# Operands of the token mixer turned by transposing DMA in 16-bit halves instead of by TensorE

## The chip, the cores and the metric

One core of one Trainium2 chip runs the whole program; the metric is device time in microseconds, the median of several runs. Kernel before: 970.59 us, median of 3 runs (971.54, 965.90, 970.59).

## The reference, cut to what matters

Two layers, each `x += 1/2 FFN1; x += mixer; x += 1/2 FFN2`, on x of 256 tokens by 1024 channels, float32; a last RMSNorm follows. The part around the change is the mixer:

```python
h  = rmsnorm(x, norm_mix[l]);  proj = h @ w_in[l]
dq, dk, dv, rq, rk, rv, rg = split(proj)      # dq, dk, dv, (rq|rk), rv, rg: 512 columns each
# group A: 4 heads, two softmax maps each, over q k^T with an ALiBi bias
s = einsum('bhcqd,bhckd->bhcqk', q, k) * scale + bias ; p = softmax(where(causal, s, -inf))
o_diff = head_rms((p[:,0] - lam * p[:,1]) @ v) * g * (1 - lam_init)
# group B: retention, 4 heads, over rq rk^T with a decay per head; gated by silu(rg)
x = x + concat(o_diff, silu(rg) * o_ret) @ w_out[l]
```

q k^T contracts over the 64 channels of a head, so TensorE needs q and k with channels on the partitions, while the projection leaves them with tokens on the partitions. Each of dq, dk and the retention pair (rq|rk) is therefore a [256 tokens x 512] float32 matrix that has to be turned, in two halves of 128 tokens (`tt` = 0, 1), four 128x128 blocks in each.

## The kernel before, in words

The order of the work is written out by hand, one instruction stream for each engine, tied by counting semaphores. SyncE (`sp`) loads weight pieces of 128x2048 float32 (1 MB; some of the last ones are 128x1024) in a ring of three raw buffers: a load waits until VectorE is through with the piece three before it (`lo_done`). ScalarE rounds each piece to its high part (`split_hi`, line 356), VectorE subtracts to get the low part (`split_lo`, line 582), and TensorE makes each product in three matmuls (lines 853 to 855) of 128x512. The mixer's column groups are c = 0 to 5 (dq, dk, dv, rqk, rv, gate); `block_of(c, tt)` is 24 matmuls into the PSUM bank `gu[tt]`, and may only start when ScalarE has read the bank's last use (`read_proj`, line 484, which counts `proj_read`).

In the mixer, ScalarE's stream goes: pieces 2 and 3, `read_proj(0, 0)`, piece 4, `read_proj(0, 1)`, piece 5, `read_proj(1, 0)`, piece 6, `read_proj(1, 1)`, piece 7, `read_proj(2, 0)`, piece 8, `read_proj(2, 1)`, and then the softmax exponentials between further pieces. VectorE makes the low parts of the same pieces. TensorE turns the four halves of dq and dk in the middle of blocks (1,0), (1,1), (2,0) and (2,1): the helper `qk_T` calls `transposes` (line 977), four 128x128 transposes into `tp[tt]`; VectorE copies each to `qT` or `kT` (`read_qkT`, line 709). Then `scores(0)` and `scores(1)` (line 988) come, and blocks (3,0), (3,1). The two halves of rqk are turned in the same way ahead of block (4,1), eight transposes in all, and are used after that block (lines 1046 and 1047).

The FFNs already turn their hidden activations by DMA: GpSimd parts a float32 tile of 128x256 into two planes of 16-bit words (`turn_out`, line 256, a copy of 128x512 uint16), ScalarE's queue issues a transposing DMA (`turn`, line 415), and GpSimd joins the turned planes again (`turn_back`, line 262). In the mixer GpSimd has nothing to do but a few narrow operations.

Of the kernel before, what the change touches and what calls it, by code (L numbers as in the profile page):

```python
# [17 lines left out]
U16 = mybir.dt.uint16  # L18
# [3 lines left out]
P = 128  # L22
D, SEQ, DEPTH = 1024, 256, 2
TT = SEQ // P
# [4 lines left out]
HEADS = 4  # L29
# [10 lines left out]
PROJ = 6  # L40
# [13 lines left out]
def build(nc, x_in, norm_ffn1, w1_gate, w1_up, w1_down, norm_mix, w_in, lam_q1, lam_k1, lam_q2, lam_k2,  # L54
          subln, w_out, norm_ffn2, w2_gate, w2_up, w2_down, norm_final, out):
    ctx = ExitStack()
    with ctx:
# [3 lines left out]
        def sem(name):  # L61
            return ctx.enter_context(nc.semaphore(name))
# [12 lines left out]
        hid = sb("hid", [P, 1024])  # L75
# [12 lines left out]
        halves = kT[:, 0:2, :].rearrange("p a n -> p (a n)").bitcast(U16).rearrange("p (t h n) -> p t h n", t=TT, h=2)  # L88
        halvesT = kT[:, 2:4, :].rearrange("p a n -> p (a n)").bitcast(U16).rearrange("p (t h n) -> p t h n", t=TT, h=2)
        hidT = qT[:, 2:4, :]  # L90
        lams = qT[:, 0:2, :].rearrange("p a (b n) -> p (a b) n", b=2)
        gsub2 = sb("gsub2", [P, DEPTH, V])
        gsub = sb("gsub", [P, V])
# [8 lines left out]
        dq_dk = wide  # L102
# [41 lines left out]
        halves_done, hidT_done, dT_hi_done, dT_lo_done = (sem(n) for n in ("halves_done", "hidT_done", "dT_hi_done", "dT_lo_done"))  # L144

        proj_ready, proj_read = sem("proj_ready"), sem("proj_read")
        qkT_psum, qkT_done = sem("qkT_psum"), sem("qkT_done")
        scores_ready, max_done, negmax_done, exp_done, rec_steps, probs_part, probs_done = (
            sem(n) for n in ("scores_ready", "max_done", "negmax_done", "exp_done", "rec_steps", "probs_part", "probs_done"))
        probsT_psum, probsT_done, pv_ready, o_sq_done, o_rstd_done, o_done = (  # L150
# [85 lines left out]
        def _(pool):  # L236
            def entry(q, tt):

                pool.wait_ge(sq_done, TT * q + tt + 1)
                nc.gpsimd.tensor_scalar(tmp[:, tt:tt + 1], ssq[:, tt:tt + 1], 1.0 / D, EPS, ALU.mult, ALU.add).then_inc(rstd_tmp, 1)  # L240
                pool.wait_ge(rstd_tmp, TT * q + tt + 1)
                nc.gpsimd.tensor_tensor(rstd[:, tt:tt + 1], tmp[:, tt:tt + 1], neg_half[:, 0:1], ALU.pow).then_inc(rstd_done, 1)
# [81 lines left out]
            for l in range(DEPTH):  # L324
                nc.gpsimd.tensor_scalar(gsub2[:, l, :], gsub2[:, l, :], 1.0 - LAM_INIT[l], None, ALU.mult).then_inc(lam_sums, 1)

            def mixer_and_ffn2_entry(layer):
                for tt in range(TT):
                    entry(3 * layer + 1, tt)
                for pair in range(2):  # L330
                    head_factor(layer, pair, o_sq_done, 2 * layer + pair + 1, o_rstd_done)
                for tt in range(TT):
                    head_factor(layer, 2 + tt, ro_sq_done, 2 * layer + tt + 1, ro_rstd_done)
                for tt in range(TT):
                    entry(3 * layer + 2, tt)
# [16 lines left out]
        def _(act):  # L352
# [125 lines left out]
            def mixer(layer):  # L478
                def read_proj(c, tt, dst, func=ACT.Copy):
                    if tt == 0:  # L480
                        act.wait_ge(proj_ready, PROJ * layer + c + 1)
                    else:
                        act.wait_ge(slot_free, SLOTS + LP * layer + MIX0 + (2 * c + 2 if c < PROJ - 1 else W0))
                    nc.scalar.activation(dst, gu[tt][:, :], func, scale=rstd[:, tt:tt + 1]).then_inc(proj_read, 1)

                def exps(h):
                    act.wait_ge(negmax_done, HEADS * layer + h + 1)
                    for t, (a, b) in enumerate(((0, 256), (256, 384))):
                        for c in range(2):
                            i = (h % 2) * 4 + 2 * t + c  # L490
                            ins = nc.scalar.activation(z(h, c, a, b), z(h, c, a, b), ACT.Exp, bias=nmx[:, i:i + 1],  # L491
                                                       accum_out=sums[:, i:i + 1])
                    ins.then_inc(exp_done, 1)

                def read_probsT(h):
                    act.wait_ge(probsT_psum, HEADS * layer + h + 1)
                    nc.scalar.activation(probsT(h, 0, 384), tp[h % 2][:, 0:384], ACT.Copy).then_inc(probsT_done, 1)
# [5 lines left out]
                def prep(pos, n=PIECE):  # L503
                    split_hi(layer, MIX0 + pos, 0, n)

                act.wait_ge(rstd_done, TT * (3 * layer + 1) + TT)
                prep(2)
                for c, dst in enumerate((dq_dk[:, :, 0:512], dq_dk[:, :, 512:1024], dv[:, :, :])):
                    for tt in range(TT):
                        prep(2 * c + 3 + tt)  # L510
                        read_proj(c, tt, dst[:, tt, :])
                act.wait_ge(lam_sums, 7)
                own = bass.ds(2 * layer, 2)
                nc.scalar.activation(lam_exp[:, own], lam_dot[:, own], ACT.Exp).then_inc(lam_exped, 1)
                for tt in range(TT):
                    prep(9 + tt, PIECE if tt == 0 else PIECE // 2)
                    exps(tt)
                    read_proj(3, tt, rqk[:, tt, :])
                read_probsT(0)
                read_probsT(1)  # L520
                for tt in range(TT):
                    prep(11 + tt, PIECE // 2)
# [56 lines left out]
        def _(dve):  # L579
# [123 lines left out]
            def mixer(layer):  # L703
                def prep(pos, n=PIECE):
                    split_lo(layer, MIX0 + pos, 0, n)

                def read_qkT(n, dst):
                    dve.wait_ge(qkT_psum, 6 * layer + n + 1)
                    nc.vector.tensor_copy(dst, tp[n % 2][:, :].rearrange("p (k n) -> p k n", k=4)).then_inc(qkT_done, 1)

                def biased_max(h):

                    dve.wait_ge(scores_ready, HEADS * layer + h + 1)
# [44 lines left out]
                    dve.wait_ge(mT_hi_done, 4 * layer + n + 1)  # L758
                    lo_of(dst, src[:, :].rearrange("p (k n) -> p k n", k=4), hi, mT_lo_done)

                for n in (2, 3, 4):
                    prep(n)
                for n, t in enumerate((qT, qT, kT, kT)):
                    prep(5 + n)
                    read_qkT(n, t[:, :, (n % 2) * P:(n % 2 + 1) * P])
                biased_max(0)
                biased_max(1)
                dve.wait_ge(lam_exped, layer + 1)
# [9 lines left out]
                    dve.wait_ge(probsT_psum, HEADS * layer + h - 1)  # L778
                    biased_max(h)
                prep(11, PIECE // 2)  # L780
                for tt in range(TT):
                    read_qkT(4 + tt, rT[:, :, tt * P:(tt + 1) * P])
                probs(2)
                prep(12, PIECE // 2)
                probs(3)
# [64 lines left out]
        def _(pe):  # L850
# [114 lines left out]
            def mixer(layer):  # L965
# [14 lines left out]
                def four(src):  # L980
                    return [src[:, i * P:(i + 1) * P] for i in range(4)]
# [29 lines left out]
                            todo.append((bank[:, (2 * t + hh) * V:(2 * t + hh + 1) * V], pairs))  # L1011
                    causal(todo, pv_ready)

                def qk_T(c, tt):

                    pe.wait_ge(proj_read, n_read + 2 * c - 1 + tt)
                    if c == 2:
                        pe.wait_ge(qkT_done, 6 * layer + tt + 1)
                    transposes(tp[tt], four(dq_dk[:, tt, (c - 1) * 512:c * 512]), qkT_psum)

                block_of(0, 0, lambda: enter_T(q, 1))
                block_of(0, 1)
                for c in (1, 2):
                    for tt in range(TT):
                        block_of(c, tt, lambda: qk_T(c, tt))
                pe.wait_ge(qkT_done, 6 * layer + 4)
                scores(0)
                scores(1)
# [5 lines left out]
                    pe.wait_ge(negmax_done, HEADS * layer + h - 1)  # L1034
                    scores(h)
                block_of(4, 0)
                for tt in range(TT):
                    pe.wait_ge(proj_read, n_read + 7 + tt)
                    pe.wait_ge(probsT_done, HEADS * layer + tt + 1)
                    transposes(tp[tt], four(rqk[:, tt, :]), qkT_psum)  # L1040
                block_of(4, 1)
                pe.wait_ge(qkT_done, 6 * layer + 6)
                pe.wait_ge(negmax_done, HEADS * layer + 4)
                for h in range(HEADS):
# [2 lines left out]
                    nc.tensor.matmul(acc[h][:, SEQ:384], rT[rows, 2 + h // 2, P:SEQ], rT[rows, h // 2, P:SEQ],  # L1047
                                     start=True, stop=True).then_inc(ret_ready, 1)
                pe.wait_ge(proj_read, n_read + 10)
                diff_out(0, gu[1])  # L1050
                transpose_probs(2)
                transpose_probs(3)
# [72 lines left out]
```

## Time and profile before

| What | Value |
|---|---|
| Median of 3 runs | 970.59 us (965.90 to 971.54) |
| The profiled execution's own time | 965.77 us |
| Its span, first to last instruction | 963.9 us |
| TensorE busy | 946.2 us, 98% of the span |
| VectorE / ScalarE / GpSimd busy | 557.4 / 458.8 / 204.6 us |
| Mean granted TensorE clock | 0.996 of full |

The span is the time from the first to the last instruction of one execution. The matmul records overlap, so a busy TensorE tells that it was never without work, not how fast it went: what a group of matmuls is worth is read from the distance between the starts of its neighbours. The mixer of layer 0 lies between about 199 and 290 us of the span, that of layer 1 some 471 us later with the same pattern.

### The profile page before, as it was taken

The page shows a single profiled execution, that of the slowest core. Times are in us where ns is not written, and L with a number is a line of the kernel's source. Part 1 is how long each engine was busy: PE and PEld are TensorE (multiplying, and loading weights), DVE is VectorE, ACT ScalarE, POOL GpSimd, SP SyncE. Part 2 cuts the span into 40 slices and gives each one's busy share as a digit, 9 for nine tenths or more (in the row PEclk, how much of TensorE's full clock was granted, in tenths as well). Part 3 has the DMA queues.
Part 4 walks back from the last instruction along what each step waited for, and adds up shares of the span by engine and source line. Part 5 has one row for each costly group of instructions (what it writes and reads, how often), then busy time and mean ns, then how long its engine had stood idle before and what let it go on. Part 6 is the DMA issues. An engine that isn't in the chain of part 4 may idle for free.

```text
span 963.9 us, 12565 instructions
## 1 busy us (share of the span) xinstructions
PE 946.2 (98%) x4365; PEld 783.3 (81%) x4365; DVE 557.4 (58%) x623; ACT 458.8 (48%) x580; POOL 204.6 (21%) x237
## 2 busy tenths in 40 slices
PE   7899999999999999999999999999999999999997
PEld 6688888888888888888888888888888888888885
DVE  5454655657575666455655555466665755555554
ACT  6343444446573444344544444444656545444442
POOL 4452521000020331221023113210001024311210
PEclk9999999999999999999999999999999999999999
DMA  7789677635344777666747867664624647867651
GB/s 266 193 199 243 219 213 226 220 124 186 132 141 165 197 236 223 201 212 213 230 124 210 256 187 229 187 224 169 217 89 175 217 114 204 270 187 221 192 165 45
DMA packets 166051, 185.98 MB, mean 193 GB/s; under 512 B 49264, under 2 KB 139424, under 8 KB 166016
## 3 DMA queue, kind: packets, MB, share of 16 engines
q1 hardware_dynamic: 121936, 173.56, 54.4%
q10 hardware_dynamic: 43760, 11.05, 6.5%
q0 software_dynamic: 320, 0.92, 0.7%
q8 instruction: 21, 0.34, 0.2%
q14 instruction: 14, 0.11, 0.0%
HBM read 173.96 MB, written 1.05 MB: 182 GB/s over the span
## 4 chain that ended last, share of the span: by engine, by line
PE 93%; ACT 2%; DVE 2%; DMA 1%; POOL 1%; issue 1%; ACTq 0%; POOLq 0%; DVEq 0%
PE gu L853 20%; PE gu L855 20%; PE gu L854 20%; PE acc L855 10%; PE acc L853 10%; PE acc L854 10%; PE tp L977 1%; PE tp L871 1%; ACT w_hi L356 1%; DVE w_lo L582 1%; DMA kT<-kT 1%; PE acc L988 1%; PE tp L1000 1%; ACT wide L491 0%; DMA rv<-in_norm_ffn_dram 0%
## 5 line engine op out<-in xcount | busy, mean ns | idle before, releaser
L582 DVE TENSOR_TENSOR w_lo<-raw,w_hi 128x2048 fp32r<-128x2048 f32 (+1 forms) x164 | 374.5, 2288 | 153.6 <-ACT w_hi L356 153.4
L853 PE MATMUL gu<-w_hi,xT_hi 128*128 128x512 f32 x896 | 352.3, 393 | 6.9 <-DVE w_lo L582 3.5
L855 PE MATMUL gu<-w_hi,xT_lo 128*128 128x512 f32 x896 | 349.6, 390 | 0.0
L854 PE MATMUL gu<-w_lo,xT_hi 128*128 128x512 f32 x896 | 349.3, 390 | 0.0
L356 ACT ACTIVATE w_hi<-raw 128x2048 fp32r<-128x2048 f32 (+1 forms) x164 | 305.4, 1866 | 15.8 <-DMA raw<-in_w_in_dram 9.1
L853 PEld LDWEIGHTS gu<-w_hi,xT_hi 128*128 128x128 f32 x896 | 168.6, 188 | 43.3 <-DVE w_lo L582 4.8
L855 PEld LDWEIGHTS gu<-w_hi,xT_lo 128*128 128x128 f32 x896 | 168.5, 188 | 35.4
L854 PEld LDWEIGHTS gu<-w_lo,xT_hi 128*128 128x128 f32 x896 | 168.7, 188 | 34.0
L853 PE MATMUL acc<-w_hi,aT_hi 128*128 128x512 f32 x384 | 150.7, 393 | 0.0
L855 PE MATMUL acc<-w_hi,aT_lo 128*128 128x512 f32 x384 | 149.7, 390 | 0.0
L854 PE MATMUL acc<-w_lo,aT_hi 128*128 128x512 f32 x384 | 149.5, 389 | 0.0
L410 ACT ACTIVATE hid<-gu,st 128x256 f32<-128x256 f32 x88 | 41.7, 474 | 225.1 <-PE gu L855 184.9
L256 POOL COPY kT<-hid 128x512 uint16<-128x512 uint16 x80 | 60.8, 761 | 310.6 <-DVE hid L650 310.6
L262 POOL COPY qT<-kT 128x512 uint16<-128x512 uint16 x80 | 100.5, 1263 | 119.1 <-issue 84.6
L650 DVE SCALAR_TENSOR_TENSOR hid<-gu,st,hid 128x256 f32<-128x256 f32 x88 | 42.4, 482 | 126.4 <-ACT hid L410 126.3
L420 ACT ACTIVATE aT_hi<-qT 128x256 fp32r<-128x256 f32 x80 | 33.4, 417 | 130.8 <-POOL qT L262 130.7
L855 PEld LDWEIGHTS acc<-w_hi,aT_lo 128*128 128x128 f32 x384 | 72.1, 188 | 15.1
L853 PEld LDWEIGHTS acc<-w_hi,aT_hi 128*128 128x128 f32 x384 | 72.1, 188 | 14.9 <-DVE aT_lo L610 0.3
L854 PEld LDWEIGHTS acc<-w_lo,aT_hi 128*128 128x128 f32 x384 | 72.1, 188 | 14.6
L610 DVE TENSOR_TENSOR aT_lo<-qT,aT_hi 128x256 fp32r<-128x256 f32 x80 | 36.1, 451 | 44.1 <-ACT aT_hi L420 44.1
L240 POOL TENSOR_SCALAR st<-st 128x1 f32<-128x1 f32 x14 | 5.5, 396 | 188.8 <-ACT rT L387 188.8
L392 ACT ACTIVATE xT_hi<-wide 128x512 fp32r<-128x512 f32 x24 | 14.8, 632 | 61.1 <-DVE wide L630 61.1
(123 smaller groups left out, 426.2 us busy)
## 6 DMA issues: line engine op xcount, KB each, us to landing
raw<-in_w_down_dram SPq DMA_DIRECT2D x88, 512.0 KB, 4.0
raw<-in_w_gate_dram SPq DMA_DIRECT2D x84, 512.0 KB, 4.0
raw<-in_w_up_dram SPq DMA_DIRECT2D x84, 512.0 KB, 5.0
raw<-in_w_in_dram SPq DMA_DIRECT2D x40, 512.0 KB, 4.8
raw<-in_w_out_dram SPq DMA_DIRECT2D x16, 512.0 KB, 4.0
raw<-in_w_in_dram SPq DMA_DIRECT2D x16, 256.0 KB, 2.9
raw<-in_w_gate_dram SPq DMA_DIRECT2D x8, 256.0 KB, 4.0
raw<-in_w_up_dram SPq DMA_DIRECT2D x8, 256.0 KB, 4.7
```

What stands on the lines that cost most here:

```text
L256: nc.gpsimd.tensor_copy(halves[:, tt, :, :], hidden[:, tt, :].bitcast(U16).rearrange("p (n h) -> p h n", h=2)).then_inc(halves_done, 1)
L262: nc.gpsimd.tensor_copy(hidT[:, tt, :].bitcast(U16).rearrange("p (n h) -> p h n", h=2), halvesT[:, tt, :, :]).then_inc(hidT_done, 1)
L356: nc.scalar.activation(w_hi[:, pos % SLOTS, 0:n], raw[:, pos % RAW, 0:n], ACT.Copy).then_inc(hi_done, 1)
L392: nc.scalar.activation(xT_hi[:, 4 * half:4 * half + 4, tt * P:(tt + 1) * P], wide[:, tt, half * 512:(half + 1) * 512].rearrange("p (k n) - ...
L410: nc.scalar.activation(silu_g[:, tt, :], gu[tt][:, 0:CH], ACT.Silu, scale=rstd[:, tt:tt + 1]).then_inc(silu_done, 1)
L420: nc.scalar.activation(aT_hi[:, 2 * par:2 * par + 2, tt * P:(tt + 1) * P], hidT[:, tt, :].rearrange("p (k n) -> p k n", k=2), ACT.Copy).th ...
L582: nc.vector.tensor_tensor(w_lo[:, pos % SLOTS, 0:n], raw[:, pos % RAW, 0:n], w_hi[:, pos % SLOTS, 0:n].bitcast(F32), ALU.subtract).then_in ...
L610: nc.vector.tensor_tensor(dst, src, hi.bitcast(F32), ALU.subtract).then_inc(done, 1)
L650: nc.vector.scalar_tensor_tensor(hidden[:, tt, :], gu[tt][:, CH:2 * CH], rstd[:, tt:tt + 1], silu_g[:, tt, :], ALU.mult, ALU.mult).then_in ...
L853: nc.tensor.matmul(out_, s_hi, m_hi, start=first, stop=False)
L854: nc.tensor.matmul(out_, s_hi, m_lo, start=False, stop=False)
L855: return nc.tensor.matmul(out_, s_lo, m_hi, start=False, stop=last)
```

## The change

Dq, dk and rqk are turned by transposing DMA, as the FFNs do it, at double the size (128x1024 16-bit words in each half). TensorE's 24 transposes of each layer and VectorE's six copies go. GpSimd gets six partings (`qk_out`) and six joins (`qk_back`) in each layer, in the order q0, q1, k0, k1 parted, q0, q1, k0, k1 joined, r0, r1 parted, r0, r1 joined. ScalarE gets six `turn`s in each layer, each of which waits for its parting and then issues the DMA. Dq and dk have buffers of their own, in tiles that are free then (`rv`, `gate`, `hid`, `rqk`). The wait for the first two turned probability maps moves to just ahead of `diff_out(0)`.

```diff
+        q_halves, q_halvesT = half_words(flat(rv)), half_words(flat(gate))
+        k_halves, k_halvesT = half_words(hid[:, :]), half_words(flat(rqk))
+        r_halves, r_halvesT = k_halves, q_halvesT
...
+        qkT_loaded = [[sem(f"{n}T_loaded{i}") for i in range(TT)] for n in "qkr"]
...
         # GpSimd
+            def qk_out(layer, c, n, tt, src, dst):
+                pool.wait_ge(proj_read, 2 * PROJ * layer + 2 * c + tt + 1)
+                nc.gpsimd.tensor_copy(dst[:, tt, :, :], src[:, tt, :].bitcast(U16).rearrange("p (n h) -> p h n", h=2)).then_inc(qk_halves_done, 1)
+            def qk_back(layer, n, tt, src, dst):
+                pool.wait_ge(qkT_loaded[n][tt], 16 * layer + 16)
+                nc.gpsimd.tensor_copy(dst[:, :, tt * P:(tt + 1) * P].bitcast(U16).rearrange("p k (n h) -> p h k n", h=2),
+                                      src[:, tt, :, :].rearrange("p h (k n) -> p h k n", k=4)).then_inc(qkT_done, 1)
...
+                for tt in range(TT):
+                    qk_out(layer, 0, 0, tt, dq_dk[:, :, 0:512], q_halves)
+                for tt in range(TT):
+                    qk_out(layer, 1, 1, tt, dq_dk[:, :, 512:1024], k_halves)
+                for tt in range(TT):
+                    qk_back(layer, 0, tt, q_halvesT, qT)
+                for tt in range(TT):
+                    qk_back(layer, 1, tt, k_halvesT, kT)
+                for tt in range(TT):
+                    qk_out(layer, 3, 2, tt, rqk, r_halves)
+                for tt in range(TT):
+                    qk_back(layer, 2, tt, r_halvesT, rT)
...
         # ScalarE
+                def turn(i, tt, src, dst):
+                    act.wait_ge(qk_halves_done, 6 * layer + 2 * i + tt + 1)
+                    act.sem_inc(halves_seen, 1)
+                    act.dma_start(dst[:, tt, :, :].rearrange("p h (k n) -> p (h k) n", k=4),
+                                  src[:, tt, :, :].rearrange("p h n -> p (h n)"), transpose=True).then_inc(qkT_loaded[i][tt], 16)
                 for c, dst in enumerate((dq_dk[:, :, 0:512], dq_dk[:, :, 512:1024], dv[:, :, :])):
                     for tt in range(TT):
                         prep(2 * c + 3 + tt)
+                        if (c, tt) == (0, 1):
+                            turn(0, 0, q_halves, q_halvesT)
+                        if (c, tt) == (1, 0):
+                            turn(0, 1, q_halves, q_halvesT)
+                        if (c, tt) == (1, 1):
+                            turn(1, 0, k_halves, k_halvesT)
+                        if (c, tt) == (2, 0):
+                            turn(1, 1, k_halves, k_halvesT)
                         read_proj(c, tt, dst[:, tt, :])
...
                     exps(tt)
+                    if tt:
+                        turn(2, 0, r_halves, r_halvesT)
                     read_proj(3, tt, rqk[:, tt, :])
                 read_probsT(0)
+                turn(2, 1, r_halves, r_halvesT)
                 read_probsT(1)
...
         # VectorE
-                for n in (2, 3, 4):
+                for n in range(2, 9):
                     prep(n)
-                for n, t in enumerate((qT, qT, kT, kT)):
-                    prep(5 + n)
-                    read_qkT(n, t[:, :, (n % 2) * P:(n % 2 + 1) * P])
...
-                for tt in range(TT):
-                    read_qkT(4 + tt, rT[:, :, tt * P:(tt + 1) * P])
...
         # TensorE
-                        block_of(c, tt, lambda: qk_T(c, tt))
+                        block_of(c, tt)
                 pe.wait_ge(qkT_done, 6 * layer + 4)
                 scores(0)
...
-                for tt in range(TT):
-                    pe.wait_ge(proj_read, n_read + 7 + tt)
-                    pe.wait_ge(probsT_done, HEADS * layer + tt + 1)
-                    transposes(tp[tt], four(rqk[:, tt, :]), qkT_psum)
                 block_of(4, 1)
                 pe.wait_ge(qkT_done, 6 * layer + 6)
...
                 pe.wait_ge(proj_read, n_read + 10)
+                pe.wait_ge(probsT_done, HEADS * layer + 2)
                 diff_out(0, gu[1])
```

## Rows read from the trace of the kernel before

**Rows 1.** The page: busy time of each engine; the chain by engine.
```profile
PE 946.2 (98%) x4365; PEld 783.3 (81%) x4365; DVE 557.4 (58%) x623; ACT 458.8 (48%) x580; POOL 204.6 (21%) x237
PE 93%; ACT 2%; DVE 2%; DMA 1%; POOL 1%; issue 1%; ACTq 0%; POOLq 0%; DVEq 0%
```
**Rows 2.** Instructions by time, TensorE, mixer of layer 0: start us, duration us, engine, line.
```profile
204.71 0.39 PE L855 MATMUL gu<-w_hi,xT_lo 128*128 128x512 f32 x1
...
210.15 0.39 PE L855 MATMUL gu<-w_hi,xT_lo 128*128 128x512 f32 x1
...
213.12 0.60 PE L977 MATMUL tp<-ident,wide 128*128 128x128 f32 x4
...
219.05 0.60 PE L977 MATMUL tp<-ident,wide 128*128 128x128 f32 x4
...
234.15 1.58 PE L988 MATMUL acc<-kT,qT 64*128 64x256 f32 x16
...
260.94 0.71 PE L1046 MATMUL acc<-rT 64*128 64x256 f32 x4
```
**Rows 3.** The chain of waits, in order of time: start us, us, what.
```profile
254.68 0.87 PE tp L977 x8
```
**Rows 4.** Instructions by time, ScalarE, mixer of layer 0.
```profile
209.53 0.67 ACT L484 ACTIVATE wide<-gu,st 128x512 f32<-128x512 f32 x1
210.09 1.91 ACT L356 ACTIVATE w_hi<-raw 128x2048 fp32r<-128x2048 f32 x1
211.90 0.68 ACT L484 ACTIVATE wide<-gu,st 128x512 f32<-128x512 f32 x1
217.28 1.92 ACT L356 ACTIVATE w_hi<-raw 128x2048 fp32r<-128x2048 f32 x1 [4.70 <-DMA raw<-in_w_in_dram]
219.10 0.67 ACT L484 ACTIVATE wide<-gu,st 128x512 f32<-128x512 f32 x1
...
222.43 0.69 ACT L484 ACTIVATE wide<-gu,st 128x512 f32<-128x512 f32 x1 [0.61 <-PE gu L855]
...
246.88 0.69 ACT L484 ACTIVATE rqk<-gu,st 128x512 f32<-128x512 f32 x1 [2.05 <-PE gu L855]
```
**Rows 5.** Instructions by time, VectorE, mixer of layer 0.
```profile
207.85 6.70 DVE L582 TENSOR_TENSOR w_lo<-raw,w_hi 128x2048 fp32r<-128x2048 f32 x3 [3.21 <-ACT w_hi L356]
219.23 2.29 DVE L582 TENSOR_TENSOR w_lo<-raw,w_hi 128x2048 fp32r<-128x2048 f32 x1 [4.68 <-ACT w_hi L356]
221.44 0.68 DVE L709 COPY qT<-tp 128x512 f32<-128x512 f32 x1
```
**Rows 6.** GpSimd's FFN parting (line 256) and join (line 262): duration ns min/median/max.
```profile
L256 POOL COPY kT<-hid x80: 611/617/2745, 24.0 to 930.5; 128x512 uint16<-128x512 uint16 x80
...
L262 POOL COPY qT<-kT x80: 762/774/2917, 29.3 to 933.8; 128x512 uint16<-128x512 uint16 x80
```
**Rows 7.** Instructions by time around 502 us: GpSimd's two, then VectorE's one.
```profile
502.27 0.62 POOL L256 COPY kT<-hid 128x512 uint16<-128x512 uint16 x1 [3.40 <-DVE hid L650]
502.82 2.83 POOL L262 COPY qT<-kT 128x512 uint16<-128x512 uint16 x1
...
502.55 2.47 DVE L582 TENSOR_TENSOR w_lo<-raw,w_hi 128x2048 fp32r<-128x2048 f32 x1 [0.45 <-ACT w_hi L356]
```
**Rows 8.** The FFN's transposing DMA: landing (median us); issue, and ScalarE behind it.
```profile
kT<-kT ACTq DMA_TRANSPOSE x80, 3.3
...
498.98 1.22 ACTq L415 DMA_TRANSPOSE kT<-kT  x1
500.24 0.47 ACT L410 ACTIVATE hid<-gu,st 128x256 f32<-128x256 f32 x1 [0.86 <-issue]
```
**Rows 9.** TensorE at the program's start by time, then one window: busy us of five engines, granted clock, DMA.
```profile
10.97 0.50 PE L853 MATMUL gu<-w_hi,xT_hi 128*128 128x512 f32 x1 [3.35 <-DVE w_lo L590]
...
12.31 0.63 PE L854 MATMUL gu<-w_lo,xT_hi 128*128 128x512 f32 x1
...
10.00:20.00 10.00, 9.03 (x37) 7.39 (x38) 7.06 (x9) 6.77 (x9) 1.31 (x2) 0.83 1.03 353
```

More of the change, by code:

```diff
@@ L90, in build, with half_words, flat @@
         hidT = qT[:, 2:4, :]
+        def half_words(t):
+            return t.bitcast(U16).rearrange("p (t h n) -> p t h n", t=TT, h=2)
+        def flat(t):
+            return t[:, :, :].rearrange("p t n -> p (t n)")
+        q_halves, q_halvesT = half_words(flat(rv)), half_words(flat(gate))
+        k_halves, k_halvesT = half_words(hid[:, :]), half_words(flat(rqk))
+        r_halves, r_halvesT = k_halves, q_halvesT
         lams = qT[:, 0:2, :].rearrange("p a (b n) -> p (a b) n", b=2)
@@ L146, in build @@
         proj_ready, proj_read = sem("proj_ready"), sem("proj_read")
-        qkT_psum, qkT_done = sem("qkT_psum"), sem("qkT_done")
+        qk_halves_done, qkT_done = sem("qk_halves_done"), sem("qkT_done")
+        qkT_loaded = [[sem(f"{n}T_loaded{i}") for i in range(TT)] for n in "qkr"]
         scores_ready, max_done, negmax_done, exp_done, rec_steps, probs_part, probs_done = (
@@ L705, in prep @@
                     split_lo(layer, MIX0 + pos, 0, n)
-                def read_qkT(n, dst):
-                    dve.wait_ge(qkT_psum, 6 * layer + n + 1)
-                    nc.vector.tensor_copy(dst, tp[n % 2][:, :].rearrange("p (k n) -> p k n", k=4)).then_inc(qkT_done, 1)
                 def biased_max(h):
@@ L1012, in diff_out @@
                     causal(todo, pv_ready)
[L1014 to L1019, printed above, removed]
                 block_of(0, 0, lambda: enter_T(q, 1))
```

## The prediction

> **What bounds the kernel now.** The page comes first: TensorE is busy for 98% of the span and makes 93% of the chain that ended last [rows 1], so time goes only where TensorE's own stream gets longer or shorter, or where it is made to wait. Next, TensorE by time in the mixer: 24 plain matmuls take 210.15 - 204.71 = 5.44 us, and there is no gap up to the scores at 234.15 [rows 2]. Then the other engines in the same stretch, with one question: how late may each be? ScalarE reads the first bank by 210.20 and the second by 212.58; it waits for a weight piece until 217.28, and reads dk's halves at 219.10 and 222.43 [rows 4]. VectorE subtracts pieces 2 to 4 without a break from 207.85 to 214.55 [rows 5]. GpSimd is free. So the mixer is TensorE's, and the change moves work from it to a chain of three engines.
>
> **What goes.** From one group of four transposes to the next 219.05 - 213.12 = 5.93 us pass [rows 2], 0.49 more than 24 plain matmuls. Four such groups are 1.96 us. The eight rqk transposes are 0.87 us of the chain [rows 3], and some 0.1 for the refill. TensorE saves 2.9 us in a layer, 5.8 in both. VectorE's six copies of 0.68 us [rows 5] go too; its waits hide them, so they count nothing.
>
> **What comes, by size.** A parting or join has double the words of the FFN's. Doubling the 617 and 774 ns medians [rows 6], less 0.05 to 0.1 for the fixed part, gives 1.2 and 1.45 us; not under 0.62 and 0.77, and more only where the copy is held up. The FFN's turn keeps ScalarE's queue for 1.21 us and lands 3.3 us after its issue starts; the activation behind the issue does not begin until it is over [rows 8]. The new turn has eight blocks of 128x128 words, not four: 1.21 to 2.42 us of issue. I take 2.4, since the work is told off by blocks, and 4.5 us to landing.
>
> **The port.** A GpSimd copy has a median of 0.77 us and a maximum of 2.92, and so far the excess is one subtraction of VectorE [rows 6]. The case at 502 us tells who goes first: the parting ends at 502.89, the join is next in line at once, but the subtraction that began to wait at 502.55 runs first, and the join takes 2.83 us [rows 7]. The two exclude each other, in turns. A piece costs a waiting copy 2.2 us.
>
> **The path through a layer** (layer 0's times; layer 1 repeats the pattern). dq's first half is read at 210.2, in the middle of VectorE's three pieces. If GpSimd gets its turn at the next change of piece, parting q0 runs from 212.35 to 213.55. ScalarE, done with piece 4 at 212.0, waits; it issues from 213.7 to 216.1, and `read_proj(0, 1)`, which ended at 212.58, now ends at 216.8. Block (1,1) needs that bank. Without its hook, (1,0), which starts 5.44 / 24 = 0.23 behind the matmul at 210.15, ends at 210.38 + 5.44 = 215.8, so TensorE waits 1.2 us. Parting q1 ends at 218.0, its turn is issued from 218.05 to 220.5, dk's first half is read by 221.15. VectorE holds the port with piece 5 until 221.5; parting k0 ends at 222.7, its turn at 225.15, dk's second half is read by 225.9, parting k1 ends at 227.1. TensorE is not held again by the banks: (2,0) starts at 222.5 and (2,1) at 227.9, which ends at 233.3.
>
> GpSimd starts its four joins only at 227.1: 5.8 us of its own. Pieces 7 and 8 reach VectorE at 227.7 and 232.1, and take a turn each, 4.4 us. The last join ends at 227.1 + 5.8 + 4.4 = 237.3. The last turn, issued at 227.15, has landed at 231.7, long before. TensorE is free at 233.3 and waits 4.0 us. A gap of 3.35 us at the start, the only one of that size, was followed by matmuls of 0.63 us instead of 0.39, at the lower of the clock's two levels; the mean granted clock of 0.83 over those 10 us [rows 9] is 3.4 us at half, 1.7 us lost. I count 1.5 here too, after the scores.
>
> **Behind the scores.** The turn of r0 stands behind `exps(1)` and ahead of `read_proj(3, 1)`: ScalarE had 2.05 us of idle there [rows 4]. The turn of r1 delays `read_probsT(1)` and piece 11 by about 3.5 us; neither is wanted before blocks of 5.4 us are through. r's last join comes some 5 us ahead of its use, at 260.94 before [rows 2]. All this I cost at nothing; if that cover fails, the stall stands in front of line 1046, and 1 to 2 us in a layer come on top. Each turn has 256 KB more on the DMA engines; a weight piece that lands a microsecond later than 217.28 [rows 4] would move the whole chain by less than that, as ScalarE already waits there for q1's parting.
>
> **Sum for a layer:** -2.9 + 1.2 + 4.0 + 1.5 = +3.8 us; for two, +7.6. Against the profiled execution's own 965.77 us (span 963.9, 1.9 around it) that is 973.4. The median of the runs, 970.59, is 4.8 above that execution; on its footing the sum gives 978.2.
>
> **A rule to weigh.** The FFN's turn lands in 3.3 us for four blocks, 0.8 us a block with everything [rows 8]. The Trainium skill, page "VectorE: DVE Perf Modes", section "The three transpose paths", has 1309 ns for a 128x128 16-bit block by DMA and 390 ns by TensorE, and its rules tell authors to take TensorE where PSUM will do. An estimate by that figure: if eight blocks went one after the other the last turn would land 10.5 us after its issue, at 237.7, the last join would end at 239.2, and the sum would be 1.9 us more in a layer. By the row it is not: four blocks would already take 5.2 us, and they land in 3.3.
>
> **The rivals.**
> Port free (12%). GpSimd's joins run one behind the other, or the pieces come too late to get between. Then the last join ends at 232.9, inside block (2,1), no clock is lost, and a layer is -2.9 + 1.2 = -1.7: 967.2 us on the median's footing; with short issues too, -2.9, 964.8. For it: the median FFN copy is within 12 ns of the shortest [rows 6]. Against it: the turn-taking at 502 us.
> Half of it (25%). The stall is there, but the clock holds, or one piece gets between and not two: +2.3 a layer without the clock, about 0 with one piece. That is 970.6 to 975.2. For it: only one gap of such length is in the trace.
> Longer issue or lost port (23%), the other side of a per cent. Parting q0 loses at the changes of piece too and runs only behind 214.55, or the issue takes longer than by blocks: the place is `turn(0, 0)`, a wait in ScalarE's stream ahead of `read_proj(0, 1)`. Losing the port once puts the chain off by 2.2 us, the last join at 239.1 to 239.5, a layer at +5.7: 982.0. It decides against me from 1.1 us a layer on. Each us that every issue takes beyond 2.4 adds about 4 to a layer: 990.
> The forecast has the other 40%, its own range 974 to 982.
>
> **How the numbers follow.** A comparison of this kernel tells about 1%, 9.7 us, from no change. Faster by more than that cannot come from 5.8 us of savings: 2%. Slower by more takes the third rival (23%) and the upper edge of the forecast (7%): 30%. Within: 68%. The range goes from the case of the free port (967) to the lost port with a slightly longer issue (987), leaving out one in ten at each end. Predicted: 978.
>
> **What would show it.** Right: no line 977 on `wide` in blocks (1,0) to (2,1); GpSimd copies of 128x1024 at 1.2 and 1.45 us where free, over 3 us where a line 582 runs; ScalarE's new issues near 2.4 us; a gap of about 1 us ahead of block (1,1) and about 4 us ahead of line 988, released by GpSimd's last join; matmuls 0.43 apart after it. Wrong: no gap at 988, joins that follow one another in 1.45 us steps, or an issue of 1.2 us; a gap at line 1046 would be a step that I costed at nothing.

## The result, and the profile after

The changed kernel takes 984.21 us (median of 6 runs, 979.9 to 989.1) against 967.02 us before (median of 6, the three runs above among them): ratio 1.0181, interval 1.0159 to 1.0203. It is 1.8% slower, inside the stated range, in the direction that was forecast, and by more than twice the amount: 17.2 us, where the sum had 7.6. The profiled execution is the slowest of the six, 989.14 us; its span of 987.1 us is 23.2 more than before, so what follows explains a loss that is some 5 us larger than the median one.

The page of the changed kernel, the two lines that answer to [rows 1]:

```profile
PE 947.3 (96%) x4317; PEld 782.1 (79%) x4317; DVE 550.8 (56%) x611; ACT 459.1 (47%) x580; POOL 250.4 (25%) x261
PE 85%; DMA 5%; ACT 3%; POOL 2%; DVE 2%; ACTq 2%; issue 1%; SPq 0%; POOLq 0%; DVEq 0%
```

TensorE's share of the chain fell from 93% to 85%, while DMA's rose from 1% to 5%, ScalarE's queue's from 0 to 2% and GpSimd's from 1% to 2%. Its own waits, of the whole program (who waited for what, us in total, times, longest), the two that the kernel before did not have:

```profile
PE acc L1029 <- POOL kT L345: 17.2, 2, 12.4
PE gu L894 <- ACT wide L517: 5.2, 3, 2.5
```

Line 1029 is the scores, line 345 the joins of k. The same waits by time (start us, duration us, in brackets the idle time before), with the scores of head 2, and those of layer 1:

```profile
222.77 0.50 PE L894 MATMUL gu<-w_hi,xT_hi 128*128 128x512 f32 x1 [1.53 <-ACT wide L517]
...
231.00 0.50 PE L894 MATMUL gu<-w_hi,xT_hi 128*128 128x512 f32 x1 [2.50 <-ACT wide L517]
...
241.56 0.80 PE L1029 MATMUL acc<-kT,qT 64*128 64x256 f32 x2 [4.80 <-POOL kT L345]
...
257.47 0.70 PE L1029 MATMUL acc<-kT,qT 64*128 64x256 f32 x4
...
726.24 1.22 PE L1029 MATMUL acc<-kT,qT 64*128 64x256 f32 x4 [12.42 <-POOL kT L345]
...
742.14 0.70 PE L1029 MATMUL acc<-kT,qT 64*128 64x256 f32 x4
```

All of the 23 us lies in the two mixers. A mixer can be read from TensorE's first transpose of x that belongs to it to the first of the FFN behind it. Kernel before, then the changed one, layer 0:

```profile
194.96 0.49 PE L871 MATMUL tp<-ident,x 128*128 128x128 f32 x3
...
301.42 0.38 PE L871 MATMUL tp<-ident,x 128*128 128x128 f32 x2
```
```profile
194.75 0.49 PE L912 MATMUL tp<-ident,x 128*128 128x128 f32 x3
...
310.61 0.38 PE L912 MATMUL tp<-ident,x 128*128 128x128 f32 x2
```

That is 106.5 us before and 115.9 after. Layer 1, read in the same way:

```profile
665.65 0.38 PE L871 MATMUL tp<-ident,x 128*128 128x128 f32 x2
...
772.10 0.38 PE L871 MATMUL tp<-ident,x 128*128 128x128 f32 x2
```
```profile
674.98 0.38 PE L912 MATMUL tp<-ident,x 128*128 128x128 f32 x2
...
795.22 0.38 PE L912 MATMUL tp<-ident,x 128*128 128x128 f32 x2
```

There it is 106.5 and 120.2. The sum of both differences, 9.4 + 13.8, is the 23.2 of the span.

Why k's joins came late shows on ScalarE's queue and on the DMA's side. ScalarE by time, layer 0 (the issues of the turns of q0, q1, k0, k1):

```profile
213.13 1.30 ACTq L542 DMA_TRANSPOSE gate<-rv  x1
...
216.81 5.17 ACTq L542 DMA_TRANSPOSE gate<-rv  x1
...
223.91 6.30 ACTq L542 DMA_TRANSPOSE rqk<-hid  x1
...
232.15 2.06 ACTq L542 DMA_TRANSPOSE rqk<-hid  x1
```

And the DMA issues of the page's kind (count, median us from issue to landing), where [rows 8] had 3.3 us for the FFN's:

```profile
kT<-kT ACTq DMA_TRANSPOSE x80, 3.3
gate<-rv ACTq DMA_TRANSPOSE x4, 14.9
rqk<-hid ACTq DMA_TRANSPOSE x4, 14.5
gate<-hid ACTq DMA_TRANSPOSE x4, 3.1
```

The turns of the retention operand, of the same size, land in 3.1 us; those of q and k take almost five times as long. They fly together with the mixer's weight loads, and these alone kept the engines fully busy from 213 to 219 us in the kernel before. What the DMA engines moved in that stretch, 219 to 225 us, before and after, with the six us ahead of it from the kernel before (the last three columns are granted clock, mean busy share of the 16 DMA engines, GB/s; where records of packets overlap the share passes 1):

```profile
213.00:219.00 6.00, 6.00 (x30) 4.92 (x29) 1.55 (x1) 1.72 (x1) 0.00 (x0) 1.00 1.00 365
219.00:225.00 6.00, 6.00 (x30) 4.94 (x29) 5.74 (x5) 5.18 (x5) 0.00 (x0) 1.00 0.60 210
```
```profile
219.00:225.00 6.00, 4.47 (x20) 3.36 (x19) 2.42 (x2) 2.49 (x2) 1.04 (x1) 1.00 1.03 79
```

The engines are fully busy, and move 79 GB/s instead of 210. This is the worst stretch of the two layers: in layer 1 it is 169 GB/s at a busy share of 1.25 from 698 to 704 us. This is what the experiments had to explain.

### The profile page after: what moved, and what is told of

It is laid out like the page before. It is cut to its first block, busy times and chain, and to the rows that moved or that the text cites. A ratio compares the mean times of both kernels' runs of the same rounds, so it can differ in the third digit from the quotient of the medians.

```text
span 987.1 us, 12497 instructions
## 1 busy us (share of the span) xinstructions
PE 947.3 (96%) x4317; PEld 782.1 (79%) x4317; DVE 550.8 (56%) x611; ACT 459.1 (47%) x580; POOL 250.4 (25%) x261
## 4 chain that ended last, share of the span: by engine, by line
PE 85%; DMA 5%; ACT 3%; POOL 2%; DVE 2%; ACTq 2%; issue 1%; SPq 0%; POOLq 0%; DVEq 0%
PE gu L894 18%; PE gu L896 18%; PE gu L895 18%; PE acc L894 9%; PE acc L896 9%; PE acc L895 9%; DMA rqk<-hid 3%; ACT w_hi L389 2%; ACTq L542 2%; DVE w_lo L632 1%; PE acc L1029 1%; PE tp L912 1%; DMA raw<-in_w_in_dram 1%; DMA kT<-kT 1%; ACT rT L420 1%
## 5 line engine op out<-in xcount | busy, mean ns | idle before, releaser
L272 POOL COPY qT<-kT 128x512 uint16<-128x512 uint16 x80 | 107.0, 1346 | 121.3 <-issue 82.5
```

The lines of the kernel that those rows point to most:

```text
L272: nc.gpsimd.tensor_copy(hidT[:, tt, :].bitcast(U16).rearrange("p (n h) -> p h n", h=2), halvesT[:, tt, :, :]).then_inc(hidT_done, 1)
```

## The experiments

Each was timed against the kernel before on the same chip; ratios are to that, with their 95% interval. "Landing" is from a DMA's issue to its completion.

**Thinned loads.** Is it the traffic beside the turns, their own size, or GpSimd's port?

```diff
+                        if thin:    # pieces 5 to 9 of each mixer
+                            d, src = d[:, 0:1, 0:128], src[:, 0:1, 0:128]
```

> The changed kernel with the mixer's weight pieces 5 to 9, the ones loaded while dq and dk are turned, loaded to an eighth (half the packets, each a quarter long); the rest of those pieces holds old data, so this part of the computation is left out. Theory A (turns and weight loads in flight together slow each other): turns of dq and dk land in 3 to 4 us instead of 13 to 19, their issues take 1.3 us each instead of up to 6.8, the gap ahead of the scores is under 1 us, and the time is 960 to 966 us against 967 before, ratio 0.993 to 1.000. Theory B (a turn of eight blocks, or two of them on the queue, is slow by itself): landings stay over 10 us and the ratio near 1.015. Theory C (GpSimd's port, as predicted): landings short, but a gap of 3 to 4 us stays, ratio 1.005 to 1.008.

Measured: 961.83 us, ratio 0.9952 (0.9933 to 0.9971).

Its DMA issues of q's and k's turns:

```profile
gate<-rv ACTq DMA_TRANSPOSE x4, 3.1
rqk<-hid ACTq DMA_TRANSPOSE x4, 3.1
```

And what is left of TensorE's waits for k's joins:

```profile
PE acc L1031 <- POOL kT L347: 0.8, 1, 0.8
```

With nothing but the traffic changed, the 22 us of waits are down to one of 0.8, and the issues take 1.25 us each. Theory A holds. B falls. Of C's stall of 3 to 4 us, 0.8 us in one layer is left: the port holds the joins up, but hardly TensorE. The thinned pieces also land early themselves, so this run does not tell late turns from late weights.

**Split turns.** Each turn as two DMAs of the size of the FFN's.

```diff
-                    act.dma_start(dst[:, tt, :, :]..., src[:, tt, :, :]..., transpose=True).then_inc(qkT_loaded[i][tt], 16)
+                    for h in range(2):
+                        act.dma_start(dst[:, tt, h, :]..., src[:, tt, h, :], transpose=True).then_inc(qkT_loaded[i][tt], 16)
```

> The changed kernel with each turn issued as two DMAs of four blocks, the size that the FFN's turns have, with everything else as it is. Theory B (the size of one turn): each lands in 3 to 4 us, as the FFN's, and the time falls to 970 to 975 us. Theory A (the sum of both traffics): the same 16-bit words beside the same loads, so the second DMA of a pair lands after 12 us or more, and the ratio to before stays at 1.013 to 1.022.

Measured: 982.82 us, ratio 1.0169 (1.0126 to 1.0212); the halves of q and k land in 8.4 and 7.9 us at the median (3.8 to 7.7 in layer 0, 9.2 to 15.5 in layer 1), where those of the retention operand take 2.5, and TensorE still waits ahead of the scores for 13.3 us in all. The landings are shorter than theory A had them, but the time did not fall: size is not the cause.

**The retention operand alone.** Q and k back on TensorE, as before the change.

```diff
-                        block_of(c, tt)
+                        block_of(c, tt, lambda: qk_T(c, tt))
...
-                    qk_out(...) / qk_back(...) and turn(...) of q and k
```

> Dq and dk turned by TensorE again as before the change, only the retention operand by DMA. Its turns landed in 3.1 us in the changed kernel and caused no wait of TensorE. Theories A and B alike: no new gap, TensorE saves eight transposes in a layer, 0.96 us, so 1.9 us in all: ratio 0.998 (0.996 to 1.000), about 965 us. If the retention part has a hidden cost (the turn of r1 ahead of the second probability map, piece 11 later), the ratio is over 1.000.

Measured: 966.16 against 965.63 us, ratio 1.0001 (0.9984 to 1.0018). In its profile each mixer is 0.9 us shorter than before (105.5 and 105.6 us), as the eight transposes should give, and landings are 3.1 us. The total does not show it. In this one profile the FFN behind the second mixer has a wait that the kernel before had not:

```profile
798.05 0.50 PE L885 MATMUL acc<-w_hi,aT_hi 128*128 128x512 f32 x1 [2.31 <-DVE aT_lo L644]
```

Whether that is what the other runs lose is not settled: one profile shows one run, and the runs of either kernel spread over 6 to 8 us.

**Held loads.** Keep the loads away from the turns.

```diff
+                        if 2 * c + h == 7:    # SyncE
+                            for n in range(2):
+                                for tt in range(TT):
+                                    sp.wait_ge(qkT_loaded[n][tt], 16 * layer + 16)
...
-                        prep(2 * c + 3 + tt)    # ScalarE: piece 7 now behind read_proj(2, 0)
```

> The changed kernel with SyncE holding weight piece 7 and all later ones until the four turns of dq and dk have landed; ScalarE takes piece 7 after it has read the first bank of dv instead of before, so that it does not wait for a load that waits for a turn. Theory A: q's turns still meet pieces 5 and 6 and land in 5 to 10 us, k's land in 3 to 5; the gap ahead of the scores falls from 4.8 and 12.4 us to 0 to 3; time 962 to 970 us, ratio 0.995 to 1.003. Theory B: landings over 10 us remain and the loads are late as well: slower than the changed kernel, ratio over 1.02.

Measured: 981.40 us, ratio 1.0151 (1.0127 to 1.0175). The landings do what theory A says, q 6.3 and k 3.1 us at the median, and TensorE does not wait for k's joins. But the time that I expected, 962 to 970 us, is wrong: the held pieces are late themselves, which theory A's figure left out.

TensorE's waits in its profile that stand for that, transposes behind VectorE's maps and FFN matmuls behind a low part:

```profile
PE tp L1025 <- DVE wide L796: 10.6, 6, 3.7
...
PE gu L901 <- DVE w_lo L639: 7.7, 5, 2.9
```

**Turns from SyncE's queue.** Is the loss in the landings, or in ScalarE being held by the issues?

```diff
+                        if at == 6: turn(layer, 0, 0, q_halves, q_halvesT)    # SyncE, behind load 6
+                        if at == 7: turn(layer, 0, 1, ...)                    # and so on at 8, 9, 12, 13
...
-                        turn(...)    # all six on ScalarE
```

> The changed kernel with all six turns of a layer issued from SyncE's queue, each behind the weight load next to it (pieces 6, 7, 8, 9, 12, 13), instead of from ScalarE's. It tells what of the loss is ScalarE being held by issues of up to 6.8 us. Theory A1 (the landing is the loss; who issues is nothing): landings stay at 10 to 19 us and the gap ahead of the scores stays at 4 to 12 us, only the two gaps of 1.5 and 2.5 us ahead of blocks (1,1) and (2,1) go: 976 to 982 us, ratio 1.011 to 1.017. Theory A2 (ScalarE's hold is the loss, since it makes the parting of k late): with ScalarE free, dk is read 3 to 7 us earlier, and the time falls to 968 to 974 us.

Measured: 966.50 us, ratio 1.0002 (0.9983 to 1.0021). Neither theory foresaw it: the landings themselves fell, as its DMA issues show.

```profile
gate<-rv SPq DMA_TRANSPOSE x4, 7.1
rqk<-hid SPq DMA_TRANSPOSE x4, 6.6
```

The same turns, beside the same loads, on the same 16 DMA engines, now issued from the queue that carries the loads. The stretch of 219 to 225 us:

```profile
219.00:225.00 6.00, 6.00 (x28) 4.95 (x28) 3.79 (x2) 3.33 (x3) 4.93 (x4) 1.00 1.10 361
```

361 GB/s instead of 79, at about the same busy share. So traffic as such is not the cause either; that it comes from two queues is. Not all of the stall is gone: TensorE waits for k's joins for 3.5 us in all, and the two mixers together are only 0.3 us shorter than before.

**q only.** Half as many turns at a time.

```diff
-                        block_of(c, tt)
+                        block_of(c, tt, (lambda: k_T(tt)) if c == 2 else None)
```

> Only dq and the retention operand are turned by DMA, dk by TensorE as before. The two turns of dq still meet pieces 5 to 7. If any turn beside the weight loads is slow (theory A by overlap), they land in 8 to 15 us, the last join ends between 227 and 234 us in layer 0, and the gap ahead of the scores is 0 to 2 us: ratio 0.997 to 1.003. If the slowness needs four turns that queue up behind one another, they land in 4 to 7 us, no gap, the mixer 1.9 us shorter in a layer, ratio 0.996 to 0.998.

Measured: 973.05 us, ratio 1.0091 (1.0053 to 1.0129); q's turns land in 11.3 us at the median, as expected for any overlap: two turns suffice. The price was under-estimated by about 1%. Gaps of 2.6 and 3.6 us stay ahead of the scores, and it is not q's joins that end them. The profile puts them down to VectorE's copy of k, and in layer 0 q's last join is over at 229.8. ScalarE and VectorE ahead of the gap:

```profile
229.44 1.92 ACT L385 ACTIVATE w_hi<-raw 128x2048 fp32r<-128x2048 f32 x1 [2.61 <-DMA raw<-in_w_in_dram]
...
231.40 2.29 DVE L624 TENSOR_TENSOR w_lo<-raw,w_hi 128x2048 fp32r<-128x2048 f32 x1 [2.21 <-ACT w_hi L385]
233.60 0.68 DVE L804 COPY kT<-tp 128x512 f32<-128x512 f32 x1
```

The copy stood behind a low part, that behind a high part, and that behind a weight piece that came late. So the turns cost time in two ways, by landing late and by making the loads late.

**Fewer packets, smaller packets.** What of the loads does it?

```diff
+                            d, src = d[:, 0:1, :], src[:, 0:1, :]          # half the packets, 2 KB
+                            d, src = d[:, :, 0:128], src[:, :, 0:128]      # all packets, 512 B
```

> As the kernel with thinned loads, but pieces 5 to 9 of the mixer are loaded to a half, in half as many packets of the full 2 KB; the other half holds old data and is left out of the computation. With an eighth of the bytes the turns landed in 3.1 us. If the loss grows with the time that the load's packets hold the DMA engines (half of it here), the turns land in 4 to 8 us and the time is 963 to 970 us. If the collapse starts as soon as there are 2 KB packets beside a turn, they still land in over 10 us, ratio over 1.010.

> Pieces 5 to 9 of the mixer are loaded to a quarter of the bytes in the full number of packets, 512 B each (a packet took 27 ns against 84 ns for 2 KB); the rest of them holds old data and is left out of the computation. If the number of packets that take turns with a turn's 1024 packets sets its landing, the turns land in over 8 us as in the changed kernel. If it is the bytes (the time that the packets hold the engines, a third here), they land in 3 to 5 us and the time is 961 to 965 us.

Measured: 962.68 us, ratio 0.9956 (0.9941 to 0.9972), with landings of 4.2 and 4.1 us; and 961.38 us, ratio 0.9952 (0.9933 to 0.9972), with 3.2 and 3.3 us. All packets at a quarter of the bytes do no harm, and half of them at full size little. The loss grows with the volume of the loads in flight, not with the number of their packets. In the profile of the small packets the first mixer is 103.66 us, 2.8 less than before: the 2.9 of saved transposes, with nothing lost. The second, with a wait of 0.8 us for k's joins, is 1.9 less.

**Turns first.** SyncE's queue, with q1, k0 and k1 ahead of loads 8 and 9.

```diff
-                        load(layer, 0, MIX0 + 2 * c + h, srcs, kk * 512)    # SyncE
+                        if at == 8:
+                            turn(layer, 0, 1, ...), turn(layer, 1, 0, ...), turn(layer, 1, 1, ...)
+                        load(layer, 0, MIX0 + 2 * c + h, srcs, kk * 512)
```

> As the kernel with all turns on SyncE's queue, but the turns of q1, k0 and k1 stand ahead of the loads of pieces 8 and 9, which have over 15 us of slack. With one queue the turns landed in 6.1 to 8.6 us behind those loads. Expected: k's turns land in 3 to 5 us, the last join of k ends by 230.5 in layer 0, ahead of the end of block (2,1) near 231.9, no gap ahead of the scores, and the mixer is 2.8 us shorter in a layer: 959 to 963 us, ratio 0.993 to 0.997. If the joins (5.5 us of copies and the subtractions between them) are the bound now, a gap of 1 to 2 us stays and the ratio is 0.997 to 1.000. If time saved in the mixer is given back in the FFNs as in the kernel with the retention part alone, the mixers are shorter and the ratio is near 1.000.

Measured: 967.19 against 966.94 us, ratio 1.0006 (0.9988 to 1.0025). The landings did as expected: q lands in 6.9, k in 3.7 us, and no wait for k's joins is left. The mixers did so in part: they are 104.3 and 105.7 us in the profile, 3.0 less in all, where 2.8 in each was expected. A part is lost behind the scores, where the transposes of the softmax maps now wait 3.5 us for VectorE, against 1.3 before:

```profile
PE tp L1018 <- DVE wide L789: 3.5, 4, 1.8
```

The profiled run, 963.17 us, is at the lower end of its 12 (960.8 to 970.7). The median is that of before. The granted clocks of the runs point to where the rest may have gone: their median is 0.9945 of full in these 12, and 0.997 in the 23 of the kernel before. That is 0.0025 of 967 us, by estimate 2.4 us. It is not shown to be the cause, and the profiled run was fast at 0.994. In this kernel's profile the clock also stood at its lower level for 3.4 us from 46.0 us on, in the first FFN, behind a wait of 1.8 us for a low part. For the retention operand alone the clocks do not differ (0.997 and 0.996), and no run shows where its gain goes.

**Loads on ScalarE's queue.** Is it that the queues differ, or that there are two?

```diff
+                        if (c, tt) in ((0, 1), (1, 0), (1, 1)):    # ScalarE, behind read_proj
+                            load(7 + (0, 1, 2)[2 * c + tt - 1])
-                        load(...) of pieces 7, 8, 9 on SyncE
```

> The changed kernel, turns on ScalarE's queue, with weight pieces 7, 8 and 9 of the mixer issued from ScalarE's queue as well, so that turns and loads share the other queue. Theory D (the collapse needs a turn and loads on two queues; on one they keep order): q0 still meets pieces 5 and 6 of SyncE's queue and lands in 6 to 10 us, the turns behind it in 3 to 9, time 966 to 975 us (ScalarE also waits for the low part of a piece before two of the loads). Theory E (SyncE's queue is the better one for turns, whatever it carries): landings of 12 us and more remain and the time is 980 us or more.

Measured: 972.74 us, ratio 1.0066 (1.0039 to 1.0092).

Its DMA issues, and then the stretch of 219 to 225 us:

```profile
gate<-rv ACTq DMA_TRANSPOSE x4, 7.6
rqk<-hid ACTq DMA_TRANSPOSE x4, 5.8
```
```profile
219.00:225.00 6.00, 6.00 (x29) 4.95 (x28) 3.00 (x2) 3.18 (x3) 1.15 (x2) 1.00 1.09 311
```

Theory D holds, E falls: ScalarE's queue turns about as fast as SyncE's when it carries the loads as well. The gaps that remain ahead of the scores, 3.8 and 3.9 us, still wait for k's joins. Two things stand ahead of these in layer 0, and no run parts them: ScalarE waits for low parts before it loads (2.8 us of idle time around the last load), and the parting of k1 and the two joins of k take 2.6 and 6.7 us beside VectorE's pieces, where 1.04 and 2.6 would do. The second is the port, as predicted.

**Two queues without a turn.** The kernel before, piece 6 of each mixer from ScalarE.

```diff
+                        if (c, tt) == (0, 1):    # ScalarE; SyncE leaves out piece 6
+                            load(6)
```

> The kernel before with one weight piece of each mixer, piece 6, issued from ScalarE's queue instead of SyncE's; it is in flight together with pieces 5 and 7 on SyncE's. No turn is near. If it takes a transposing DMA on the second queue to make both slow, the three pieces land as before, in 4.6 to 7.5 us, and the time is that of before, ratio 0.997 to 1.003. If any two queues that are full at once slow each other, they land in over 9 us.

Measured: 967.05 us, ratio 1.0001 (0.9984 to 1.0018); pieces 5 to 7 land in 4.6 to 7.3 us, against 4.6 to 7.4 before. Two plain queues do not hinder each other, as far as one piece on the second shows.

**The wait filled.** Does the idle time cost more than itself?

```diff
+                for _ in range(44 if layer == 0 else 112):
+                    nc.tensor.transpose(acc[0][:, 0:P], ident[:, :], ident[:, :])
                 pe.wait_ge(qkT_done, 6 * layer + 4)
```

> The changed kernel with dummy 128x128 transposes in TensorE's stream between block (2,1) and the wait ahead of the scores: 44 in layer 0 (about 4.8 us) and 112 in layer 1 (about 12.2 us), the length of the two gaps. Their results are overwritten. If the granted clock falls because TensorE idles, it now stays at the upper level: from the first score to the scores of head 2 it is 13.3 us in both layers as before the change, not 15.9, and the time falls by 4 to 5.5 us, to 977 to 981. If the clock's fall has nothing to do with the gap, the time stays at 983 to 985 or rises by what the dummies overrun the wait.

Measured: 986.75 us, ratio 1.0222 (1.0186 to 1.0258): the forecast of the time failed. The dummies' length is fixed and the wait's is not (the changed kernel spreads from 980 to 989 us), so they overran it: in layer 1 of the profile k's last join ended at 715.0 us, and the dummies at 721.2. But the clock is told:

```profile
721.25 0.49 PE L1029 MATMUL acc<-kT,qT 64*128 64x256 f32 x2
...
734.55 0.70 PE L1029 MATMUL acc<-kT,qT 64*128 64x256 f32 x4
```

Those are the same two instructions in layer 1 of this kernel, the first score and those of head 2: 13.3 us apart, and so they are in layer 0. Before the change it was 13.3 too, from 234.15 [rows 2] to the scores of head 2:

```profile
247.42 0.49 PE L988 MATMUL acc<-kT,qT 64*128 64x256 f32 x2
```

In the changed kernel it was 742.14 - 726.24 = 15.9, and 257.47 - 241.56 = 15.9 in layer 0. The idle wait costs 2.6 us beyond itself. Shorter waits had other prices: one of 2.6 us ahead of the scores cost nothing more (q only, layer 0), one of 2.4 cost 1.6 (turns from SyncE's queue, layer 1), and two of 3.8 and 3.9 cost 1.6 and 2.7 (loads on ScalarE's queue). In the changed kernel, behind the gap of layer 0 (the third value from the end is the granted clock: 0.50, the level of 1.2 GHz):

```profile
244.00:247.00 3.00, 3.00 (x12) 2.29 (x9) 2.86 (x19) 1.86 (x8) 0.00 (x0) 0.50 0.00 0
```

## Why the prediction was right and wrong

**The bound and the savings: right.** TensorE's stream set the time. The undisturbed mixer, layer 0 with small packets, got 2.8 us shorter; 2.9 was predicted.

**The sizes of the pieces: nearly right.** A parting that ran free took 1.04 us, a join 1.32 to 1.37; predicted 1.2 and 1.45. The port works in turns, as read at 502 us [rows 7]. Parting q0 began in the middle of VectorE's three pieces and got its turn at the next change (behind it a free parting and a free join):

```profile
210.04 2.99 POOL L340 COPY rv<-wide 128x1024 uint16<-128x1024 uint16 x1 [4.38 <-ACT wide L517]
215.23 1.04 POOL L340 COPY rv<-wide 128x1024 uint16<-128x1024 uint16 x1 [2.20 <-ACT wide L517]
...
231.99 1.37 POOL L345 COPY qT<-gate 128x1024 uint16<-128x1024 uint16 x1
```

Parting q0 ended at 213.03; predicted 213.55. Behind it I expected a wait of 1.2 us ahead of block (1,1). With an issue of 1.30 us in place of the 2.4 that I chose, there was none. The lower end of that bound, the row as it stood [rows 8], was the right one: without other traffic eight blocks are issued in 1.25 us and land in 3.1. Four blocks without other traffic land in 2.4, not in the 3.3 of the row, which is a median over turns most of which had loads beside them. The estimate by the Trainium skill's 1309 ns a block ("VectorE: DVE Perf Modes", section "The three transpose paths") gave 10.5 us for eight blocks in a row; the 3.1 us disagree with that, as the prediction held.

**The step that failed** is the 4.5 us to landing, and with it the sentence on the 256 KB more that each turn puts on the DMA engines: it reckoned with a weight piece that lands a microsecond later, and put even that at nothing. The turns of q and k landed in 13 to 19 us but for one, and the weight pieces beside them in up to 13.8 instead of 7.4. While earlier turns were under way ScalarE's issues took up to 6.8 us, where 2.4 was taken as fixed; that made `read_proj(1, 0)`, `read_proj(1, 1)` and the partings behind them late (the 5.2 us of waits for line 517), and k's turns later still.

I had taken the median landing of the FFN's turns as the price, and put them where, before the change, loads alone kept the engines busy 1.00 of the time (213 to 219 us, 365 GB/s), then 0.60. The trace of before had the warning. Its 80 FFN turns, issued by ScalarE beside SyncE's loads, are spread widely:

```profile
DMA to landing us min/median/max: 2.4/3.3/8.4
```

By its DMA packets, 26 of them had next to no load beside them and landed in 2.4 us at the median; 15 had loads that kept the engines busy 0.7 to 0.9 of the time, and landed in 5.2. A row gives a DMA's price only for the traffic that it was read in.

The gap ahead of the scores was then 4.8 and 12.4 us, where 4.0 was predicted from the port. The first figure is close by luck, for a wrong reason: with the traffic thinned, the joins and VectorE's pieces in turns left 0.8 us in one layer. What was too long there is the start of the four joins, put at 227.1; with issues of 1.25 us it came at 224.0 in that run. GpSimd's four joins in it:

```profile
224.04 4.66 POOL L347 COPY qT<-gate 128x1024 uint16<-128x1024 uint16 x2
228.60 2.64 POOL L347 COPY kT<-rqk 128x1024 uint16<-128x1024 uint16 x2
```

They take 7.2 us, the joins' own time and one piece's, where the prediction had two pieces get between, 10.2.

**The clock: right, and too small.** 1.5 us taken, 2.6 measured, in each layer. The prediction took it from the stretch behind the gap of the start [rows 9], whose mean gave 1.7; the same arithmetic turned round makes 5.2 us at half clock behind each of these gaps. That one gap costs the price of another is what failed in it: over all the runs the price lay between 0 and 2.7 us.

**The cover behind the scores: right.** The turns of r landed in 3.1 us, with hardly a load beside them, and no wait arose at lines 1076 and 1077, the retention matmuls; costed at nothing, it was nothing.

**The sum.** By terms, both layers: -5.6 saved, +17.2 and +5.2 of waits, +5.3 of clock, 22.1 of the 23.2 us; the other 1.1 is not assigned. The rival of a longer issue had the mechanism nearest to it, "Each us that every issue takes beyond 2.4 adds about 4 to a layer", though it was not every issue, and the cause, not named there, was a second queue.

**The range: held with luck.** The time is beyond the forecast's own 974 to 982 us and inside the stated 967 to 987. That range was set around a median of 970.59 us; all six runs give 967.02. The measured 17.2 us are more than the 16.4 that the range's upper end allowed above its own footing.

## What to carry to other kernels

Before you move work to DMA, look at what else the 16 DMA engines carry in that very stretch and from which queue; a landing read in a quiet stretch is no price for a busy one. Look at the longest landings of a group and not only at its median. If transposing DMAs must fly beside heavy loads, issue them from the queue that issues the loads; putting them ahead of the loads with slack brought k's landings from 6.6 to 3.7 us, but no gain in the total. And a chain of three engines that replaces 3 us of the bound engine has to be early by more than its jitter: even the best version here was no faster than the kernel before.

## What the runs showed of the hardware

A transposing DMA on one queue and full weight loads on another bring both down: 79 GB/s at a busy share of 1.03, against 361 (all on SyncE's queue) and 311 (turns and three loads on ScalarE's). It needs the turns (with one plain piece on the second queue nothing slows) and large volume (a quarter of the bytes in the same packets does no harm). The records of the packets show where the busy time goes: single packets hold an engine for longer. From 219 to 225 us the turns' packets of 256 bytes took 93 ns at the median, and 18 ns in the same stretch with the loads thinned; the loads' packets took 270 ns on the mean, though 84 at the median. What each of them waits for, no run shows. Nor does any run tell whether it takes the transposing: plain copies in packets of 256 bytes on the second queue were not tried.

The Trainium skill says, on page "DMA: Bandwidth & Descriptors", section "Rules for kernel authors", that a transpose next to ordinary DMAs needs nothing, and on page "Advanced Engine Details and Errata", section "X-Bar Transpose (TRN2)", that transposing DMAs are as fast as regular ones. For results this case has nothing against the first. The second agrees where nothing flies beside them: a turn of 256 KB landed in 3.1 us, and the mixer's weight loads of 256 KB in 3.4 at the median. For time beside other traffic the measurement decides: next to ordinary DMAs of another queue the same turn took 14.9 us at the median and not 3.1.
